# The last down projection with the tokens in the array and the weights moving

## What is computed

```python
sh1, sc1, g1, sh2, sc2, g2 = adaln(c, w_ada[1], b_ada[1])       # silu(c) @ w_ada + b_ada, six rows of 2048
xl = xl + g1 * short_conv_mixer(...)
u = dwconv3(modulate(rmsnorm(xl), sh2, sc2) @ ffn_w_up[1], ffn_conv[1])
g, v = split(u, 2)
xl = xl + g2 * ((silu(g) * v) @ ffn_w_down[1])                  # (256 x 5632) @ (5632 x 2048)
return rmsnorm(xl, final_gain)
```

## Time and profile before

| | us |
|---|---|
| median of 3 runs | 2563.17 (2559.64 to 2564.53) |
| the profiled execution | 2562.41 |
| its span, first to last instruction | 2560.7 |
| TensorE busy | 2510.0 |
| VectorE busy | 2047.4 |
| ScalarE busy | 1272.9 |
| GpSimd busy | 198.0 |

### The profile page before, as it was taken

One profiled execution on the slowest core, in us unless ns is written; L12 is line 12 of the kernel. 1 busy time (PEld: TensorE's weight loads), 2 busy tenths in 40 slices (PEclk: granted clock), 3 DMA queues, 4 the chain that ended last, 5 costly groups with the idle time before them and its releaser, 6 DMA issues.

```text
span 2560.7 us, 39781 instructions
## 1 busy us (share of the span) xinstructions
PE 2510.0 (98%) x14322; PEld 2178.7 (85%) x14322; DVE 2047.4 (80%) x2729; ACT 1272.9 (50%) x1730; POOL 198.0 (8%) x301
## 2 busy tenths in 40 slices
PE   6999999998999999999999999999999999999998
PEld 4778888777998888888888988888988888888887
DVE  6888887887898889987888799979988876765443
ACT  5422324676565555554444544445655555554443
POOL 1002221000000001100111011101000000000000
PEclk9999999999999999999999999999999999999999
DMA  9768887554778778887999699968688766665554
GB/s 352 273 222 268 301 270 222 165 163 140 242 244 270 254 257 273 287 262 228 297 288 298 228 315 328 339 223 270 214 279 269 249 188 191 187 191 187 186 187 136
DMA packets 465214, 623.53 MB, mean 243 GB/s; under 512 B 18804, under 2 KB 404246, under 8 KB 458160
## 3 DMA queue, kind: packets, MB, share of 16 engines
q1 hardware_dynamic: 424544, 450.94, 53.4%
q0 software_dynamic: 40208, 170.51, 20.6%
q10 hardware_dynamic: 320, 0.13, 0.0%
HBM read 619.41 MB, written 2.10 MB: 243 GB/s over the span
## 4 chain that ended last, share of the span: by engine, by line
PE 81%; DVE 9%; DMA 4%; ACT 4%; issue 2%; SPq 0%; ACTq 0%; DVEq 0%; POOLq 0%
PE ps L1923 47%; PE ps L1930 25%; DMA raw<-in_sconv_w_in_dram 3%; DVE w_lo L1130 3%; PE ps L1846 2%; PE ps L1848 1%; PE ps L1847 1%; ACT w_hi L622 1%; DVE ada_sum L1201 1%; DVE start_sum L1124 1%; PE ps L1981 1%; PE ps L1980 1%; PE ps L1982 1%; DVE ada_sum_b L1201 1%; DVE broad_sum L1253 1%
## 5 line engine op out<-in xcount | busy, mean ns | idle before, releaser
L622 ACT ACTIVATE w_hi<-raw 128x1024 fp32r<-128x1024 f32 (+1 forms) x800 | 820.9, 1039 | 923.0 <-PE ps L1930 720.8
L1130 DVE TENSOR_TENSOR w_lo<-raw,w_hi 128x1024 fp32r<-128x1024 f32 (+1 forms) x800 | 953.6, 1200 | 406.7 <-ACT w_hi L622 403.8
L1923 PE MATMUL ps<-xs,w_hi 128*128 128x512 f32 x3200 | 780.3, 394 | 0.5 <-DVE v_rows L1178 0.5
L1923 PEld LDWEIGHTS ps<-xs,w_hi 128*128 128x128 f32 x3200 | 587.3, 188 | 120.9 <-issue 6.9
L1930 PEld LDWEIGHTS ps<-xs,w_lo 128*128 128x128 f32 x3200 | 413.5, 191 | 17.1
L1930 PE MATMUL ps<-xs,w_lo 128*128 128x256 f32 x3200 | 420.1, 283 | 0.0
L1923 PE MATMUL ps<-act,w_hi 128*128 128x512 f32 x1408 | 340.5, 392 | 0.0
L1923 PEld LDWEIGHTS ps<-act,w_hi 128*128 128x128 f32 x1408 | 257.5, 188 | 49.2
L1930 PEld LDWEIGHTS ps<-act,w_lo 128*128 128x128 f32 x1408 | 181.6, 191 | 7.5
L1930 PE MATMUL ps<-act,w_lo 128*128 128x256 f32 x1408 | 183.9, 283 | 0.0
L1923 PE MATMUL ps<-xs_sin,w_hi 128*128 128x512 f32 x704 | 170.3, 392 | 1.3 <-ACT w_hi L622 0.9
(11 more groups left out here) (258 smaller groups left out, 2765.9 us busy)
## 6 DMA issues: line engine op xcount, KB each, us to landing
raw<-in_ffn_w_up_dram SPq DMA_DIRECT2D x352, 512.0 KB, 4.6
ada_ring<-in_w_ada_dram POOLq DMA_DIRECT2D x176, 512.0 KB, 5.1
raw<-in_ffn_w_down_dram SPq DMA_DIRECT2D x128, 512.0 KB, 4.5
raw<-in_attn_w_qkv_dram SPq DMA_DIRECT2D x96, 512.0 KB, 4.8
broad_ring<-in_w_ada_dram POOLq DMA_DIRECT2D x48, 1024.0 KB, 6.0
raw<-in_sconv_w_in_dram SPq DMA_DIRECT2D x96, 512.0 KB, 6.0
ada_ring_kv<-in_w_ada_dram POOLq DMA_DIRECT2D x48, 512.0 KB, 5.1
raw<-in_ffn_w_down_dram SPq DMA_DIRECT2D x64, 384.0 KB, 3.7
```

The source lines that it names most:

```text
L622: nc.scalar.activation(w_hi[:, slot, 0:n_tiles, :], raw[:, slot, 0:n_tiles, :], ACT.Copy).then_inc(hi_made, 1)
L1130: nc.vector.tensor_tensor(w_lo[:, slot, 0:n_tiles, :], raw[:, slot, 0:n_tiles, :], w_hi[:, slot, 0:n_tiles, :], ALU.subtract).then_inc(lo_ ...
L1923: mm(ps[:, bank + m, :], w_hi[:, slot, t, P * m:P * m + P], src[:, tile + t, :], start=(is_first and t == 0), stop=False)
```

## The change

`dn1` becomes 4 slabs of 512 output features, each 22 units of 2 tiles x 512 columns. The tokens' tile stands in the array (four pieces per tile: two halves of the tokens, high and rest) and the weights move, 512 columns at a time: for each unit 8 high matmuls and 4 low ones. The last two units of the last slab are done for the first half of the tokens and then for the second. The result has tokens on partitions. So the residual is turned to token rows during slab 0 (`turn_res`, `keep_res`), the gate g2 and the final gain become rows loaded or summed on all partitions (`gate_row`, `gain_row`), VectorE multiplies, adds and gains (`add_row`, `gain_rows`), ScalarE squares with a sum along the row (`square_row`), and the last norm needs no sums by TensorE. The third wide sum goes through matmuls with ones, which leave the sum on all partitions. `gained`, `keep_rows`, `turn_rows` and the sums with ones go. The dummy root that loads ScalarE's table moves from the end of `up1` into slab 0.

```diff
-          "sin": (24, 4), "so": (8, 4), "up1": (44, 4), "dn1": (8, 12)}
+          "sin": (24, 4), "so": (8, 4), "up1": (44, 4), "dn1": (4, 22)}
+ROW_UNITS, RES_TURNS = FT // 2, (6, 8, 10, 12, 14, 16, 18, 20)
...
+            def row_unit(n):
+                u = UNITS["dn1"] + n
+                sp.wait_ge(lo_made, u - 3)
+                tile, col = n % ROW_UNITS * 2, n // ROW_UNITS * VSLAB
+                sp.dma_start(wide[:, u % 4, :, :], dn_w[1][:, tile:tile + 2, col:col + VSLAB]).then_inc(raw_full[u % 4], 16)
...
+            pool.wait_ge(ada_step, 16 * ADA_LAST)
+            pool.dma_start(gate_row[:, :], b_ada[1][G2 * P:G2 * P + D].unsqueeze(0).broadcast_to([P, D])).then_inc(gate_loaded, 16)
             pool.wait_ge(w_used, UNITS["up1"] + 8)
             for t in range(16):
                 broad_part(2, t)
+            pool.wait_ge(w_used, UNITS["dn1"])
+            pool.dma_start(gain_row[:, :], final_gain.unsqueeze(0).broadcast_to([P, D])).then_inc(gain_loaded, 16)
...
+            def keep_res(n):
+                se.wait_ge(res_turned, n + 1)
+                nc.scalar.activation(out_tok[:, n % 2, n // 2 * VSLAB:(n // 2 + 1) * VSLAB], ps[:, 4 + n % 4, :], ACT.Copy).then_inc(res_kept, 1)
+            def square_row(slab, t):
+                n = 2 * slab + t
+                se.wait_ge(row_added, n + 1)
+                wait(se, row_squared, n)
+                nc.scalar.activation(row_squares[:, :], out_tok[:, t, slab * VSLAB:(slab + 1) * VSLAB], ACT.Square,
+                                     accum_out=red[:, 1 + t, slab:slab + 1]).then_inc(row_squared, 1)
+            for n in range(4 * ROW_UNITS):
+                slab, k = n // ROW_UNITS, n % ROW_UNITS
+                hi((UNITS["dn1"] + n) // 4, (UNITS["dn1"] + n) % 4)
+                if slab == 0:
+                    v_up_point(k, "up1", FT // 2 - 1, 1)
+                    if k == 5:
+                        up_hi("up1", FT // 2 - 1)
+                    if k == 6:
+                        nc.scalar.activation(row_rstd[:, 2:3], row_inv[:, 2:3], ACT.Sqrt)
+                    if k in RES_TURNS:
+                        keep_res(RES_TURNS.index(k))
+                elif k in (4, 5):
+                    square_row(slab - 1, k - 4)
+            square_row(3, 0)
+            square_row(3, 1)
...
+                    if b == 2:
+                        ve.wait_ge(gate_loaded, 16)
+                        row = gate_row[:, VSLAB * g:VSLAB * g + VSLAB]
+                        nc.vector.tensor_tensor(row, row, ps[:, BROAD_BANKS[g], :], ALU.add).then_inc(broad_added, 1)
+                        return
...
+            def add_row(slab, t):
+                n, cols = 2 * slab + t, slice(slab * VSLAB, (slab + 1) * VSLAB)
+                if t == 0:
+                    ve.wait_ge(row_made, slab + 1)
+                else:
+                    ve.wait_ge(w_used, UNITS["dn1"] + ROW_UNITS * (slab + 1))
+                ve.wait_ge(broad_added, 12)
+                nc.vector.tensor_tensor(gated_row[t][:, :], ps[:, 2 * (slab % 2) + t, :], gate_row[:, cols], ALU.mult).then_inc(row_read, 1)
+                ve.wait_ge(row_read, n + 1)
+                ve.wait_ge(res_kept, n + 1)
+                nc.vector.tensor_tensor(out_tok[:, t, cols], out_tok[:, t, cols], gated_row[t][:, :], ALU.add).then_inc(row_added, 1)
...
+                elif k in (2, 3):
+                    add_row(slab - 1, k - 2)
+                elif k in (7, 8):
+                    gain_rows(slab - 1, k - 7)
+            add_row(3, 0)
+            add_row(3, 1)
+            gain_rows(3, 0)
+            ve.wait_ge(row_squared, 8)
+            nc.vector.reduce_sum(row_sum[:, 0:2], red[:, 1:3, :], AX_X).then_inc(row_folded, 1)
...
+                if b == 2:
+                    mm(ps[:, BROAD_BANKS[g], :], ones[:, :], broad_sum[:, VSLAB * g:VSLAB * g + VSLAB], start=True, stop=True).then_inc(broad_reduced, 1)
+                    return
...
+            def turn_res(n):
+                pe.wait_ge(broad_added, 12)
+                wait(pe, res_kept, n - 3)
+                for c in range(4):
+                    last = nc.tensor.transpose(ps[:, 4 + n % 4, P * c:P * c + P], res[:, 4 * (n // 2) + c, P * (n % 2):P * (n % 2) + P], ident[:, :])
+                last.then_inc(res_turned, 1)
+            def row_high(slab, k, row):
+                u, bank = UNITS["dn1"] + ROW_UNITS * slab + k, 2 * (slab % 2) + row
+                for t in range(2):
+                    for part in range(2):
+                        mm(ps[:, bank, :], act[:, 2 * k + t, T * part + P * row:T * part + P * row + P], hi_wide[:, u % 4, t, :],
+                           start=(k == 0 and t == 0 and part == 0), stop=False)
+            def row_low(slab, k, row):
+                u, bank = UNITS["dn1"] + ROW_UNITS * slab + k, 2 * (slab % 2) + row
+                for t in range(2):
+                    last = mm(ps[:, bank, :], act[:, 2 * k + t, P * row:P * row + P], lo_wide[:, u % 4, t, :],
+                              start=False, stop=(k == ROW_UNITS - 1 and t == 1))
+                if k == ROW_UNITS - 1 and row == 0:
+                    last.then_inc(row_made, 1)
+                if row == 1:
+                    last.then_inc(w_used, 1)
...
+                    pe.wait_ge(hi_made, u + 1)
+                    for row in range(2):
+                        row_high(slab, k, row)
+                    pe.wait_ge(lo_made, u + 1)
+                    for row in range(2):
+                        row_low(slab, k, row)
+                    if slab == 0 and k in RES_TURNS:
+                        turn_res(RES_TURNS.index(k))
```

More of the change, by code:

```diff
@@ L465, in _ @@
             up("up1", up_w[1])
-            down("dn1", dn_w[1])
+            for n in range(4 * ROW_UNITS):
+                row_unit(n)
             for half in range(2):
@@ L470, in _ @@
                     cols = slice(D // 2 * half, D // 2 * half + D // 2)
-                    sp.wait_ge(fin_scaled[t][half], 2 if half == 1 else 1)
+                    sp.wait_ge(fin_scaled[t][half], 2 if half == 1 and t == 1 else 1)
                     sp.dma_start(out_rows[:, t, cols], out_tok[:, t, cols]).then_inc(fin_stored, 16)
@@ L491, in _ @@
                 pool.dma_start(dst, src).then_inc(vecs_loaded, 16)
-            assert len(loads) == 21
+            assert len(loads) == 20
             def ada_slab(j, layer, col, slots=ADA_SLOTS):
@@ L704, in res_point @@
                     nc.scalar.activation(part_c[:, :, :], res[:, bass.ds(2 * s, 2), :], ACT.Square).then_inc(sq_made, 1)
[L705 to L726, removed]
+                    n_norm = ("o", "dn0", "so").index(phase)
+                    for m in range(2):
+                        last = nc.scalar.activation(plain_u[n_norm][:, bass.ds(2 * s + m, 1), 0, 0:T], res[:, bass.ds(2 * s + m, 1), :], ACT.Copy,
+                                                    scale=vec[:, bass.ds(2 * s + (NORMS[n_norm][0] + m), 1)])
+                    last.then_inc(u_hi_made, 1)
             def shift_hi(n_norm):
@@ L1019, in _ @@
             up("up1", so_tail, 2)
[L1020 to L1023, removed]
+            def keep_res(n):
[7 more added lines that the diff above has]
+                                     accum_out=red[:, 1 + t, slab:slab + 1]).then_inc(row_squared, 1)
+            for n in range(4 * ROW_UNITS):
+                slab, k = n // ROW_UNITS, n % ROW_UNITS
[12 more added lines that the diff above has]
+            square_row(3, 1)
             se.wait_ge(rows_inv, 3)
             nc.scalar.activation(row_rstd[:, 0:2], row_inv[:, 0:2], ACT.Sqrt).then_inc(rows_rstd, 1)
-            se.wait_ge(fin_kept, 7)
+            se.wait_ge(row_gained, 6)
             se.wait_ge(rows_rstd, 3)
-            for half, cols in enumerate(FIN_COLS):
+            for half, cols in enumerate((slice(0, D // 2), slice(D // 2, D - VSLAB))):
                 nc.scalar.activation(out_tok[:, 1, cols], out_tok[:, 1, cols], ACT.Copy, scale=row_rstd[:, 1:2]).then_inc(fin_scaled[1][half], 1)
@@ new lines, in gain_rows @@
+            def gain_rows(slab, t):
+                cols = slice(slab * VSLAB, (slab + 1) * VSLAB)
+                ve.wait_ge(row_squared, 2 * slab + t + 1)
+                ve.wait_ge(gain_loaded, 16)
+                nc.vector.tensor_tensor(out_tok[:, t, cols], out_tok[:, t, cols], gain_row[:, cols], ALU.mult).then_inc(row_gained, 1)
+            for n in range(4 * ROW_UNITS):
+                slab, k = n // ROW_UNITS, n % ROW_UNITS
+                lo((UNITS["dn1"] + n) // 4, (UNITS["dn1"] + n) % 4)
+                if slab == 0:
+                    v_up_point(k, "up1", FT // 2 - 1, 1)
+                    if k == 4:
+                        gate_pair("up1", FT // 2 - 1)
+                    if k == 5:
+                        low_pair("up1", FT // 2 - 1)
+                elif k in (2, 3):
+                    add_row(slab - 1, k - 2)
+                elif k in (7, 8):
+                    gain_rows(slab - 1, k - 7)
@@ L1738, in _ @@
```

(29 more changed lines are left out.)

49 lines of the change are left out of this document (22 added, 27 removed).

## The result

The changed kernel takes 2573.64 us (2570.58 to 2574.12, 6 runs) against 2563.58 (6 runs of the kernel before): ratio 1.0042, 95% interval 1.0031 to 1.0052, so it is slower. Forecast were 2572.8 us and slower.

The account below looks back on a forecast made before the run. TensorE, busy 2510.0 of 2560.7 us, was taken as the bound, plus holes and the tail. Terms -6.2 + 15.9 + 2.1 - 2.2 = +9.6 on 2562.4 gave 2572.0, with 0.8 for the median 2572.8 us; range 2565 to 2580.

Parts of the forecast that it names:

- The hole: Slab 0 of the last down projection: TensorE waits for ScalarE's rounding after each of eight turns, 2.0 us each, +15.9 us.
- the 0.64 us until the copy: Step of the hole's chain: from a turn's first transpose to ScalarE's copy, 0.64 us, taken from the attention's end.
- the 0.12 us put in for the weight load: Step of the hole's chain: TensorE's weight load, otherwise hidden by the stream, estimated at 0.12 us per hole.
- The stream: TensorE's last down projection: 352 instructions fewer for the same columns, with turns added, 242.2 us against 248.36: -6.2 us.
- The step of 0.2267: Time per 512-column matmul in the new projection, taken from the V projection: 1056 of them make 239.4 us.
- The turn: Part of the stream: each group of four transposes of the residual in slab 0 takes 0.35 us, eight 2.8 us.
- The gate's sum: Third wide sum: four fp32 matmuls with ones, 3.5 us, replace four groups of transposes, 1.4 us: +2.1 us.
- The tail: Chain after TensorE's last matmul: scaling starts after 3.4 us instead of 5.70 and takes 2.2 against 2.07: -2.2 us.
- Rival A: Slab 0, after units 6 to 20: ScalarE's copies don't hold up TensorE; with no hole 2556.9 us, faster; chance 0.07.
- Rival B: Slab 0: TensorE's clock also falls, restarting at 1.2 GHz after each of eight holes; 12 us more, 2585 us; chance 0.08.

Follow-up runs that it names:

- the repaired order: The changed kernel with TensorE's eight turns of the residual four units earlier, ScalarE's program untouched: 2556.77 us, 0.9977 of the kernel before.

## Why the prediction was right

The sum was +9.6 us, the medians moved by +10.1. By its terms:

- *The hole* was +15.9 and is 15.2, with 1.9 us in place of 2.0 each: the chain of release, copy and rounding was as put together from the attention's rows, step by step, down to the 0.64 us until the copy. Only the 0.12 us put in for the weight load didn't show: the first matmul starts 0.01 us behind its load (2324.06, 2324.07). That order, not work, makes the hole: moving the turns alone takes it away, and a longer copy lengthens each.
- *The stream* was -6.2 and is 243.3 - 248.4 = -5.1. The step of 0.2267 was right. The turn was mis-sized: 0.35 us is only up to the next matmul's start, and the matmuls behind it lose another 0.12. The 2.5 ns per matmul of the Trainium skill (TensorE: Matmul & The Clock Gate, "Wait — 56ns, not 53.3ns?") don't hold for this stream, in which each matmul has a weight load of its own: splitting cost 13 ns for each added matmul.
- *The gate's sum* was +2.1. The new groups take 4 x 0.88 = 3.5 us, as forecast; the transposes they replace took 1.9 in place of 1.4: +1.6. TensorE's timeline of the kernel before shows it, with 2.29 us from group to group, eight steps of 0.2267 and 0.48:

```profile
2081.12 0.60 PE L1871 MATMUL ps<-ident,broad_sum 128*128 128x128 f32 x4
2081.47 2.10 PE L1923 MATMUL ps<-xs,w_hi 128*128 128x512 f32 x8
2083.41 0.60 PE L1871 MATMUL ps<-ident,broad_sum 128*128 128x128 f32 x4
```

- *The tail* was -2.2 and is -2.4, 3.32 us to the scaling against the 3.4 worked out.
- -5.1 + 15.2 + 1.6 - 2.4 = +9.3. That this comes within 0.3 of the sum is in part luck: the terms were off by +1.1, -0.7, -0.5 and -0.2, which nearly cancel. The profiled executions differ by 11.4; 2.0 us of that arose before the third wide sum, whose first group starts at 2071.02 in the changed kernel and at 2069.06 before. This is within the spread of executions: in the seven other runs whose program is the same up to there, it starts between 2065.71 and 2069.89.

Rival A failed in the changed kernel and is the truth of the repaired order: with it the time is 2556.8, and 2556.9 was its price, with the stream's and the gate's terms off as above. Rival B got 0.08, and its evidence against was too weak: its 2.1 us are the weight load's wait, and the two waits of that stretch at full clock, 1.87 and 2.13 us of idle matmul time, say little of eight in a row. The changed kernel kept its clock, but with holes only 0.22 us longer it fell behind five of eight; that it kept it, nothing in the prediction's working had secured. The Trainium skill (the same page, "HAM oscillation — how this bites in real kernels") tells of a loop that loses its clock in each of its waits. The run with the copy made twice agrees for seven of its eight, with 0.85 over the stretch; there a fall costs 1.6 us beside a wait of 2.1.

## What to carry to other kernels

Where two engines have work for each other inside one loop, compare where it stands in both programs: an engine that runs its program in order holds up, by one wait, all that it makes later. One unit of distance was enough here to hide 2 us. A form that saves instructions on the critical engine should be costed together with the hand-overs that it adds, each as a chain of releases from rows. A repeated hole may cost its own length today and nearly twice as much when it grows by a fifth of a microsecond: here 1.9 us became 3.7 where the clock fell.

## What the hardware showed that was not expected

Eight idle times of TensorE of 1.63 us (the last 1.72), each turn 7.80 to 7.84 us after the one before, left the granted clock at 1.00. With 1.85 us it fell behind five of eight (0.89 over the stretch), with 2.12 us behind seven of eight (0.85), to steps of 0.435 us for 512 columns, the level of 1.2 GHz. Holes of the same length had both outcomes. The tail's store time shrank when half of it was issued early, from 5.46 to 4.25 us behind the last scaling.
